# Token-major down projections and stage ends in a three-stage diffusion trunk step, without products of ones

## The reference

```python
h = rmsnorm(x, g[0]) * (1 + scale0) + shift0
x = x + 0.5 * gate0 * rmsnorm((silu(h @ Wg0) * (h @ Wu0)) @ Wd0, g[1])
h = rmsnorm(x, g[2]) * (1 + scale1) + shift1
x = x + gate1 * rmsnorm(mixer(h), g[3])      # w_in, mLSTM heads, SSD heads, w_out
h = rmsnorm(x, g[4]) * (1 + scale2) + shift2
x = x + 0.5 * gate2 * rmsnorm((silu(h @ Wg1) * (h @ Wu1)) @ Wd1, g[5])
```

## Time and profile before

| | |
|---|---|
| median of 3 runs | 3079.03 us (3078.14 to 3079.24) |
| profiled execution, its span | 3079.0 us |
| granted TensorE clock, mean | 0.993 |
| busy: TensorE, VectorE, ScalarE, GpSimd | 98%, 44%, 32%, 59% |
| bytes moved by DMA, mean rate | 531.54 MB, 173 GB/s |
| weight loads of 512 KB, issue to landing | 3.5 to 5.5 us by tensor |

### The profile page before, as it was taken

The page is one execution under the profiler, slowest core; times in us unless marked ns, Lnnn a source line. Parts: engine busy times, 40 slices in busy tenths (PEclk is TensorE's granted clock), DMA queues, the critical chain, the costliest instruction groups (busy, mean ns, idle before and its releaser), DMA issues.

```text
span 3079.0 us, 48036 instructions
## 1 busy us (share of the span) xinstructions
PE 3027.0 (98%) x17401; PEld 2859.1 (93%) x17401; DVE 1352.3 (44%) x2931; ACT 974.9 (32%) x1226; POOL 1825.1 (59%) x906
## 2 busy tenths in 40 slices
PE   6999999999999999999999999999999999999998
PEld 2899999999999998899999999899999999999998
DVE  3365566556655665876733352522343111100113
ACT  2322322232222223534332233523222322222223
POOL 2565665566556555557754545566565666566666
PEclk8999999999999999999999999999999999999999
DMA  9866675667566756655444435246554644444443
GB/s 363 280 219 197 220 225 177 206 211 232 175 207 205 232 183 199 220 161 157 138 135 128 118 106 171 73 128 190 168 179 139 143 149 129 126 126 126 126 129 109
DMA packets 494159, 531.54 MB, mean 173 GB/s; under 512 B 29275, under 2 KB 454723, under 8 KB 493123
## 3 DMA queue, kind: packets, MB, share of 16 engines
q1 hardware_dynamic: 458048, 508.62, 52.4%
q10 hardware_dynamic: 35971, 21.27, 2.5%
HBM read 519.12 MB, written 9.66 MB: 172 GB/s over the span
## 4 chain that ended last, share of the span: by engine, by line
PE 91%; DVE 2%; POOL 2%; issue 2%; DMA 1%; ACT 1%; ACTq 1%; DVEq 0%; POOLq 0%
PE banks L784 25%; PE banks L786 25%; PE banks L785 25%; PE banks L959 4%; PE banks L960 4%; PE banks L961 4%; DVE HB L2261 1%; PE banks L870 1%; POOL w_lo L2557 1%; PE banks L813 1%; PE banks L1275 0%; PE banks L1295 0%; DMA w_raw<-in_ffn_w_gate_dram 0%; ACTq L1503 0%; PE banks L1280 0%
## 5 line engine op out<-in xcount | busy, mean ns | idle before, releaser
L2557 POOL TENSOR_TENSOR w_lo<-w_raw,w_hi 128x1024 fp32r<-128x1024 f32 (+1 forms) x668 | 1595.8, 2395 | 1033.0 <-ACT w_hi L1378 1032.5
L784 PE MATMUL banks<-xn_hi,w_hi 128*128 128x384 f32 x3920 | 1329.9, 339 | 5.2 <-POOL w_lo L2557 2.1
L786 PE MATMUL banks<-xn_hi,w_lo 128*128 128x384 f32 x3920 | 1311.7, 335 | 0.0
L785 PE MATMUL banks<-xn_lo,w_hi 128*128 128x384 f32 x3920 | 1311.6, 335 | 0.0
L1378 ACT ACTIVATE w_hi<-w_raw 128x1024 fp32r<-128x1024 f32 (+1 forms) x668 | 704.2, 1057 | 1463.5 <-PE banks L786 743.8
L784 PEld LDWEIGHTS banks<-xn_hi,w_hi 128*128 128x128 f32 x3920 | 737.4, 188 | 29.4 <-issue 22.4
L785 PEld LDWEIGHTS banks<-xn_lo,w_hi 128*128 128x128 f32 x3920 | 737.4, 188 | 4.2 <-issue 3.1
L786 PEld LDWEIGHTS banks<-xn_hi,w_lo 128*128 128x128 f32 x3920 | 736.9, 188 | 0.0
L1876 DVE SCALAR_TENSOR_TENSOR banks<-w_raw,cT,banks 128x256 f32<-128x256 f32 x1372 | 548.0, 483 | 0.0
L1989 DVE TENSOR_TENSOR AM<-AM,banks 128x384 f32<-128x384 f32 x88 | 44.8, 551 | 598.1 <-PE banks L786 598.1
L784 PE MATMUL banks<-hid_hi,w_hi 128*128 128x384 f32 x704 | 235.2, 334 | 0.0
(11 more groups left out here) (293 smaller groups left out, 1819.5 us busy)
## 6 DMA issues: line engine op xcount, KB each, us to landing
w_raw<-in_w_ada_dram SPq DMA_DIRECT2D x288, 512.0 KB, 5.5
w_raw<-in_ffn_w_gate_dram SPq DMA_DIRECT2D x176, 512.0 KB, 4.4
w_raw<-in_ffn_w_up_dram SPq DMA_DIRECT2D x176, 512.0 KB, 3.9
w_raw<-in_ffn_w_down_dram SPq DMA_DIRECT2D x176, 512.0 KB, 3.7
w_raw<-in_w_in_dram SPq DMA_DIRECT2D x104, 512.0 KB, 3.7
w_raw<-in_w_out_dram SPq DMA_DIRECT2D x32, 512.0 KB, 3.5
HB<-row_wait ACTq DMA_DIRECT2D x12, 512.0 KB, 4.7
x_wait<-xT ACTq DMA_DIRECT2D x1, 3072.0 KB, 9.9
```

The costliest lines, as they stand in the source:

```text
L784: pe.matmul(out, wh, hi, start=start, stop=False)
L785: pe.matmul(out, wh, lo, start=False, stop=False)
L786: return pe.matmul(out, w_lo[:, w, off:off + P], hi, start=False, stop=stop)
L2557: pool.tensor_tensor(used(w_lo[:, slot(p), :], p), used(w_raw[:, p % NR, :], p), used(w_hi[:, slot(p), :], p).bitcast(F32), ALU.subtract). ...
```

## The change

Both the first FFN's down product and `w_out` become token-major like the second FFN's, so `y` leaves all stages with a token per partition, and x too is kept so, in `AX` (`x_tok`). At each stage end the norm goes by token (`end_of`, for all three): squares with their sums on ScalarE, gains on GpSimd, `finish` on VectorE, and squares of the new x beside it. The products of ones over squares and those of `stay_awake` are gone (`WAKE` is zero). For the next stage TensorE turns the new x tile by tile (`turn`, three transposes each, four tiles ahead of the fresh pieces that use them), and the root of x is spread over the partitions by one product of ones with a diagonal for each chunk (`spread_root`). Gate-and-gain rows are now made for each of the three stages (`store_gains`, `load_gains`). Four last pieces of each of these three products are taken by chunk (`last_of_ffn`, `last_of_out`). Splits of the first pieces of the next stage are placed among the squares and the gains. The clearing of `y` moves from the preparation into the first FFN's first part, and x doesn't need `x_keep` and L1343 any more.

```diff
-OUT_UNITS = [("A", t, OUT_PARTS[:3]) for t in range(4)] + [("F", 4, OUT_PARTS)] + [("B", t, OUT_PARTS[3:]) for t in range(4)]
...
+OUT_UNITS = [("A", cc, OUT_HALVES[:6]) for cc in range(2)] + [("F", 2, OUT_HALVES)] + [("B", cc, OUT_HALVES[6:]) for cc in range(2)]
+OUT_UNITS += [("F", 3, OUT_HALVES)]
...
-WAKE_Y, WAKE_X, WAKE_PASS = 20, 12, 12
+WAKE = ((0, 0), (0, 0))
...
-        x_tok = y[:, :, :].rearrange("p k t -> p (k t)").rearrange("p (c n) -> p c n", c=NCH)
+        x_tok = AX.rearrange("p (c n) -> p c n", c=NCH)
...
+                    for m, j in enumerate(TAIL_ORDER):
+                        load_wide(n, tail_of(n) + m, j, D_FF // P - PK)
+                    wait_pe(sp, tail_of(n) - 1)
+                    load_gains(2 * n)
+                def load_gains(stage):
+                    sp.wait_ge(g_stored, 32 * (stage + 1))
+                    for g in range(2):
+                        sp.dma_start(g_rows[stage][:, g, :], g_wait[stage, g].partition_broadcast(P)).then_inc(g_loaded, 16)
...
+                        load(P_MIX + j, w_out[:, 2 * q:2 * q + 2, 512 * t:512 * t + 512], tiles=2)
+                    if j == S_OUT + 20:
+                        sp.wait_ge(mix_ready, 2 * HEADS)
+                        sp.wait_ge(m_cstored, 64 * HEADS)
+                        load_gains(1)
...
-                def square_sum(name, k):
...
-                    pe.matmul(sum_bank(name)[:, 0:TOK], ones[:, :], sq[:, (base + k) % 2, :], start=(k == 0),
-                              stop=(k == KT - 1)).then_inc(ss_mm, 1)
...
-                def added_sum(name):
...
-                    for k in range(last, KT):
-                        square_sum(name, k)
...
+                def turn(stage, k):
+                    if k >= KT:
+                        return
+                    wait_finished(pe, stage, 2, k // 4)
+                    if k >= 2:
+                        pe.wait_ge(xt_done, KT * (stage + 1) + k - 1)
+                    for c in range(NCH):
+                        last = pe.transpose(psum[TURN_BANKS[stage][k % 2]][:, P * c:P * c + P], x_tok[:, c, P * k:P * k + P], idn[:, :])
+                    last.then_inc(x_turned, 1)
+                def spread_root(stage, c):
+                    pe.wait_ge(root_diag, NCH * stage + c + 1)
+                    pe.matmul(ROOT_BANK[:, P * c:P * c + P], ones[:, :], x_dia[:, c, :], start=True, stop=True).then_inc(root_spread, 1)
+                def last_of_ffn(n, p0):
+                    for c, cc in LAST_BLOCKS:
+                        wait_added(pe, 2 * n, c, cc - 2)
+                        for kk in range(PK):
+                            half, k = divmod(kk, 2)
+                            p = p0 + 2 * cc + half
+                            if c == 0 and k == 0:
+                                wait_lo(pe, p)
+                            last = wide_products(psum[token_bank(cc, c)], p, k, hid_hi[:, kk, P * c:P * c + P], hid_lo[:, kk, P * c:P * c + P],
+                                                 kk == 0, kk == PK - 1)
+                            if c == NCH - 1 and k == 1:
+                                last.then_inc(pe_piece, 1)
+                        if c < NCH - 1:
+                            last.then_inc(last_mm, 1)
+                def wide_products(bank, p, k, hi, lo, start, stop):
+                    wh, wl = w_hi[:, slot(p), 512 * k:512 * k + 512], w_lo[:, slot(p), 512 * k:512 * k + 512]
+                    pe.matmul(bank[:, :], hi, wh, start=start, stop=False)
+                    pe.matmul(bank[:, :], lo, wh, start=False, stop=False)
+                    return pe.matmul(bank[:, :], hi, wl, start=False, stop=stop)
...
-                    def down_piece(p, j, it, i=None, part=None):
...
-                            for k in range(PK):
-                                last = product(psum[bank][:, 0:TOK], slot(p), k * PC + f * P, hid_hi[:, k, :],
-                                               hid_lo[:, k, :], k == 0, k == PK - 1)
...
+                        if m < 4:
+                            wide_piece(tail_of(n) + m, j, FFN_IT - 1)
+                    last_of_ffn(n, tail_of(n))
...
+                for k in range(2):
+                    turn(0, k)
+                for c in range(2):
+                    spread_root(0, c)
                 pass_pieces(NR, 4 * ADA_PASS)
-                stay_awake(WAKE_PASS)
+                stay_awake(WAKE[0][1])
+                spread_root(0, 2)
+                for k in range(2, TURN_AHEAD):
+                    turn(0, k)
...
+                def last_of_out():
+                    for c in range(NCH):
+                        for j in range(S_LAST, len(SLOTS)):
+                            q, u = SLOTS[j][2], SLOTS[j][3]
+                            if c == 0:
+                                wait_lo(pe, P_MIX + j)
+                                pe.wait_ge(mix_lo, 4 * OUT_PARTS.index(q // 2) + 4)
+                            for k in range(2):
+                                ins = wide_products(psum[out_bank(NCH * (u - UNIT_OUT) + c)], P_MIX + j, k, xn_hi[:, 2 * q + k, P * c:P * c + P],
+                                                    xn_lo[:, 2 * q + k, P * c:P * c + P], False, j == len(SLOTS) - 1 and k == 1)
+                            if c == NCH - 1:
+                                ins.then_inc(pe_piece, 1)
+                        if c < NCH - 1:
+                            ins.then_inc(last_mm, 1)
                 def flip_tiles(bank, src):
...
+                        if j == 3:
+                            for c in range(3):
+                                square_block(2 * n, "y", c, 0)
+                    for c in range(3):
+                        square_block(2 * n, "y", c, 1)
...
+                    for name, c, cc in SQUARES[0][6:]:
+                        square_block(0, name, c, cc)
+                        if (name, c, cc) == ("x", 1, 0):
+                            make_hi(GATE_FIRST[0])
+                        if (name, c, cc) == ("x", 1, 1):
+                            make_hi(GATE_FIRST[1])
+                        if (name, c, cc) == ("x", 2, 0):
+                            make_hi(GATE_FIRST[2])
...
+                def store_gains(stage):
+                    act.wait_ge(g_ready, stage + 1)
+                    for g in range(2):
+                        act.dma_start(g_wait[stage, g].rearrange("(k p) -> p k", p=P), coefG[:, :, g], allow_slow_non_contiguous=True).then_inc(g_stored, 16)
...
+                def square_block(stage, name, c, cc):
+                    n_sq = square_at(stage, name, c, cc)
+                    if name == "y":
+                        wait_added(act, stage, c, cc)
+                    else:
+                        wait_finished(act, stage, c, cc)
+                    if n_sq >= 2:
+                        act.wait_ge(squared, n_sq - 1)
+                    else:
+                        act.wait_ge(norms_clear, 1)
+                    block_ = tok_block(c, cc) if name == "y" else x_block(c, cc)
+                    act.activation(y_square[:, n_sq % 2, :], block_, ACT.Square, accum_out=SUMS[name][:, c, cc:cc + 1]).then_inc(squared, 1)
+                    if cc == 3:
+                        act.wait_ge(y_biased if name == "y" else x_biased, NCH * stage + c + 1)
+                        act.wait_ge(squared, n_sq + 1)
+                        act.activation(ROOT[name][:, 0, c:c + 1], SUMS[name][:, c, 3:4], ACT.Sqrt, bias=BIAS[name][:, c:c + 1],
+                                       scale=1.0 / D).then_inc(y_std if name == "y" else x_rooted, 1)
...
                 act.dma_start(x_wait, AX).then_inc(x_spilled, 16)
+                store_gains(1)
...
+                def root_row(stage, c0, c1):
+                    dve.wait_ge(root_spread, NCH * stage + c1)
+                    link(dve.tensor_copy(x_root_rows[:, P * c0:P * c1], ROOT_BANK[:, P * c0:P * c1]))
...
+                    dve.tensor_scalar(x_dia[:, c, :], idn[:, :], ROOT["x"][:, 1, c:c + 1], None, ALU.mult).then_inc(root_diag, 1)
...
+                def gains_first(stage):
+                    dve.wait_ge(g_loaded, 32 * (stage + 1))
+                    for c in range(NCH):
+                        last = gain_first(stage, c)
+                    link(last)
...
+                    out = tok_block(c, cc) if stage == 2 else x_block(c, cc)
+                    dve.scalar_tensor_tensor(out=out, in0=gain_block(c, cc), scalar=ROOT["y"][:, 1, c:c + 1],
+                                             in1=x_block(c, cc), op0=ALU.mult, op1=ALU.add).then_inc(out_ready if stage == 2 else x_fin, 1)
...
+                def end_of(stage):
+                    def roots_of_x(c):
+                        if stage < 2:
+                            root_bias(stage, "x", c)
+                    def diagonal_of(c):
+                        if stage < 2:
+                            diagonal(stage, c)
+                    def rows_of(c0, c1):
+                        if stage < 2:
```

(55 more changed lines are left out.)

614 lines of the change are left out of this document (219 added, 395 removed).

## The result

The changed kernel takes 3104.96 us (median of 4 runs, 3102.76 to 3105.41), before 3079.14 (3078.14 to 3080.16); the ratio is 1.0083, with an interval of 1.0068 to 1.0097. The forecast was 3089 with a range to 3100: the side was right, the size 10 us where it is 26. The profiled execution spans 3103.3 us, 24.3 more than that of before.

The account below looks back on a forecast made before the run. TensorE was taken to bound the loops, and the chain of squares and finishes the passages. Savings of 25.8 us and losses of 35.6 net -9.8: 3079.0 + 9.8 = 3088.8, say 3089 us, range 3066 to 3100.

Parts of the forecast that it names:

- the first passage: First FFN's last product (ends at T) to the gates stage's first product: T + 26.8 against T + 30.6, 3.8 us saved.
- the half clock: TensorE's products at 1.2 GHz after pauses: 1.6 us lost behind the tail's stop, 2.0 for each of the two passages.
- the stop in the tail: End of first FFN: TensorE waits for gain rows, stored as 4-byte elements and loaded back, until 1209.7; 8.9 us lost.
- the second passage: w_out's last product (ends at T) to the second FFN's first: T + 17.8 instead of 30.2, 12.4 us saved.
- What bounds the kernel; the ones are only filler: TensorE bounds the loops; squares, VectorE and GpSimd bound the passages, so leaving out products of ones gives nothing by itself.
- The down products: Token-major products 512 columns wide replace those 384 wide: 7.0 us saved in the first FFN, 2.6 in w_out.
- and so does the sixteenth adaLN piece, whose slot the eighth frees (17.3 + 4.2 load + 0.5): First passage: the sixteenth adaLN piece stands in TensorE's queue ahead of the third spread, whose row copy comes at T + 23.
- The pieces behind the passages: First pieces of the next stages: turns lose 5.0 us each; later low halves lose 2.0 in the first, 2.2 in the second.
- which nothing hides when TensorE is the bound: Transposes inside the first pieces after a passage, 12 tiles of 3 at 0.42 us a tile, cost their full time: 5.0 us.
- The gates stage: `store_gains(1)`, issued behind the 3 MB spill of x, makes weight loads late: 5.0 us lost, ends 0 and 10.
- Rival (a): The tail's gain rows are in time: TensorE doesn't stop, the gates stage isn't held up; 3073.5 us, chance 0.17.
- Rival (c): The passages' whole work, 48 transposes and the first two pieces run at half clock: 3098 us, chance 0.15.

Follow-up runs that it names:

- e10: Changed kernel with turned gain store (64 rows of 512 bytes), second column block's adds ahead of `gains_first`, and the first passage's three splits earlier: 3084.1 us.
- e14: e11 with the third spread of the first passage ahead of the last eight adaLN pieces: 3074.1 us, ratio 0.9986.
- e11: e10 with the turns spread evenly, two in each piece that uses x first, six tiles ahead: 3076.9 us, ratio 0.9993.
- e6: Changed kernel with gain rows stored as 64-byte packets, source and destination both contiguous (values in another order): 3085.9 us, ratio 1.0021.
- e2: Changed kernel with idle products of ones again: 12 ahead of the first passage's third spread, 20 and 8 around the second passage: 3109.34 us, ratio 1.0101.
- e15: e14 with the second passage's splits behind the norm's own work and the last gain multiply ahead of their low halves: 3072.4 us, ratio 0.9979.
- e9: Changed kernel with VectorE's adds of the second column block ahead of `gains_first` in both tails: 3104.1 us, ratio 1.0079.
- e5: Changed kernel with only the first passage's third root spread moved ahead of the last eight adaLN pieces: 3104.7 us, ratio 1.0081.

## Why the forecast was right and wrong

The side was right: slower. The size, 24.3 us in the trace for 9.8, lacks 14.5. Put by mechanism they are: the first passage 6.3, the half clock 5.3, the stop in the tail 2.3, the second passage 1.9; the rows that came better than forecast give 1.3 back.

*What bounds the kernel; the ones are only filler.* Right in the main. Leaving them out of the kernel before changes its time by 0.08%, within the interval of nothing, though its trace has 28 products at half clock behind the passages for 3.

*The down products.* +7.0 and +2.6 forecast. The loop gave 5.7 for 6.4, and w_out's stretch 3.1, with the hole of 1.0 us (forecast 1.1) ahead of `last_of_out` in it.

*The tail.* The mechanism was right, down to its parts: store 18.0 us (17.3 forecast), loads 8.0 (7.1), released by VectorE. The term was mis-sized, 13.9 us against 10.5: the stop was 11.2 for 8.9, and 12 products at 0.43 instead of 0.227, with the dearer first one, 2.7 for 1.6; the price per product at half clock had been taken from the narrower products.

*The first passage.* This is the term "First product at T + 26.8 against T + 30.6: +3.8". The passage is 2.5 us longer than before instead, so the term is 6.3 us off. The eighth piece at T + 17.8 agrees with T + 17.3 (the text named it the sixth). The step that failed is "and so does the sixteenth adaLN piece, whose slot the eighth frees (17.3 + 4.2 load + 0.5)": it priced the last load alone. The sixteenth was issued at 1241.7, right behind the eighth's products, as forecast, but the loads from the eighth on stand behind one another, one arriving every 1.3 us, and it was worked at T + 28.4, not 22. Early splits and the third spread put ahead took the passage from 33.4 to 29.1 (e10, e14), 1.0 us that the spread turns add to it included.

*The pieces behind the passages.* The two stretches were 15.2 and 11.1 us longer, forecast 12.0 and 7.2. Counted in the traces, against before (us):

| | waits | turns | product next to a turn, and the like | products at half clock |
|---|---|---|---|---|
| gates stage, first 144 products | +6.4 | +3.5 | +0.8 | +4.5 (30 for 2) |
| its forecast | 7.0 | 5.0 | in the turns | 0 |
| second FFN's start | +3.3 | +3.0 | +1.0 | +3.7 (24 for 1) |
| its forecast | 2.2 | 5.0 | in the turns | 0 |

So the step "which nothing hides when TensorE is the bound" held: the turns cost 0.36 to 0.39 us a tile, forecast 0.42. The place of the turns, which the forecast didn't look at, makes part of the waits, since VectorE and the low halves behind it come late: with the turns spread, the waits of the gates stage fell from 3.3 to 0.2 us and those of the second FFN's start from 4.9 to 2.9 (e11 against e10).

*The clock.* The second step that failed: 1.6 + 2.0 + 2.0 = 5.6 us were charged, for the stop of the tail and the pauses of the passages. Counted, it is 2.7 + 4.5 + 3.7 = 10.9. Right behind the passages only 7 and 6 products ran at half clock, 1.5 and 1.1 us; some 6 us stand behind the holes inside the stages, which the sum priced by their idle time alone. That is an argument from the spacing of products and the granted clock; no run changed the clock by itself.

*The gates stage.* The store behind the spill cost 6.1 us (e6 against the changed kernel), forecast 5.0 by late weights. The place was right, the way partly: the weights were in their slots and ScalarE, which makes their high halves, was held 6.7 us by the issue. The other way, a transfer beside it made late, showed when the store was moved: 13.0 us.

*The second passage.* Forecast -10.4 with the clock, measured -10.5, and this is in part luck. The first product came at T + 19.6, not T + 17.8: on the way two small operations of VectorE took 2.30 and 2.18 us instead of 0.21 and 0.29, beside GpSimd's low halves. The 2.0 us of clock charged here made up for it, while the clock's own cost stands in the row behind.

*Rival (a)*, the rows in time, didn't come; made to come (e6), it took 3086, not 3073.5, since the other terms were too small. *Rival (c)*, the clock, forecast as half rate through the passages' whole work and the first two pieces, didn't come in that form; the mean granted clock is 0.983 for 0.993, with half clock behind each stop and hole. Idle products where e2 put them don't pay. The range ended at 3100 because its ends were made from the rivals, not from the terms, and the terms that failed were all too small.

What stays open: the price of the half clock was not tested by a run of its own, and the 28.1 us that e15 still waits for adaLN loads, most of them ahead of the first FFN and in the first passage, were not followed.

## What to carry to other kernels

Price a queue of loads by its rate, not by the last one: if k transfers must come behind a point, the last comes k times the spacing later. Price a hole in the busiest engine by its idle time and by the products at half clock behind it. When work moves between in-order engines, place what feeds another engine evenly in the feeder's queue; and look for the cause of a stop at what landed last, since an order that frees the bank only moved the stop by a stage (e9), and an edit that shows nothing behind a late transfer can be worth a second run once that is in time (e5 0.2 us, e14 2.8). And look at every place that an edit reaches: the one of e9 also took 1.7 us at the end of the kernel. A redesign that takes work off the busiest engine can still lose by what its new small transfers do to the queue that issues them and to the transfers beside them.
